# Nine weight slots instead of six in the expert phases of a two-layer decoder step, with the rows fetched on ACT's queue

## The reference, cut to what matters

```python
def hier_moe(x, w_group, b_group, w_router, b_router, w_gate_up, w_down):
...
    def expert_block(a):
        xb, e = a
        gate, up = jnp.split(xb @ w_gate_up[e], 2, axis=-1)
        return (jax.nn.silu(gate) * up) @ w_down[e]
...
    y = jax.ops.segment_sum(yp[dest] * w_sorted[:, None].astype(x.dtype), tok_sorted, num_segments=n)
```

## Time and profile before

| | us |
|---|---|
| timed runs, median of 3 (lowest to highest) | 2165.03 (2158.33 to 2166.91) |
| the profiled execution, first to last instruction | 2143.9 |
| PE busy in it | 1693.2 |
| expert phase of layer 0, first to last product (L883 to L896) | 648.0 to 1207.5 |
| expert phase of layer 1 | 1579.2 to 2109.5 |

### The profile page before, as it was taken

One profiled execution on the slowest core, in us unless ns is written; L12 is line 12 of the kernel. 1 busy time (PEld: TensorE's weight loads), 2 busy tenths in 40 slices (PEclk: granted clock), 3 DMA queues, 4 the chain that ended last, 5 costly groups with the idle time before them and its releaser, 6 DMA issues.

```text
span 2143.9 us, 25298 instructions
## 1 busy us (share of the span) xinstructions
PE 1693.2 (79%) x8325; PEld 773.9 (36%) x8326; DVE 487.7 (23%) x1022; ACT 324.1 (15%) x601; POOL 123.2 (6%) x147
## 2 busy tenths in 40 slices
PE   5989787687937788787887579989757887887782
PEld 3433333344432443333332244434523333322231
DVE  1679244321140110000000132120510000000003
ACT  3022344222020001000110220000210011110001
POOL 0012000120120000000000200001010000000002
PEclk7999888798968999999999879999679998999897
DMA  9951686785048698999999930201569999999995
GB/s 357 416 171 70 216 300 231 239 303 217 0 164 309 243 392 334 395 386 412 411 411 410 364 134 0 79 0 41 196 264 363 361 412 410 411 411 411 411 410 208
DMA packets 194115, 604.27 MB, mean 282 GB/s; under 512 B 15951, under 2 KB 18288, under 8 KB 193897
## 3 DMA queue, kind: packets, MB, share of 16 engines
q1 hardware_dynamic: 162800, 522.55, 62.9%
q10 hardware_dynamic: 21025, 46.17, 5.7%
q0 software_dynamic: 10208, 34.48, 4.5%
HBM read 551.57 MB, written 52.01 MB: 282 GB/s over the span
## 4 chain that ended last, share of the span: by engine, by line
PE 60%; DVE 10%; SPq 8%; DMA 8%; issue 7%; ACT 4%; POOL 1%; ACTq 1%; DVEq 0%; POOLq 0%
PE ps L883 17%; PE ps L896 10%; PE ps L1008 8%; SPq L400 7%; PE ps L578 5%; PE ps L594 3%; DMA ring<-in_w_gate_up_dram 2%; PE ps L928 2%; DMA ring<-in_w_down_dram 2%; PE ps L623 2%; PE ps L940 1%; DVE W L1483 1%; PE ps L906 1%; PE ps L520 1%; PE ps L718 1%
## 5 line engine op out<-in xcount | busy, mean ns | idle before, releaser
L883 PE MATMUL ps<-ring,W 128*64 128x512 f32 x2048 | 470.5, 610 | 55.8 <-issue 32.3
L896 PE MATMUL ps<-ring,W 128*64 128x512 f32 x1024 | 268.1, 670 | 50.3 <-DVE W L1806 48.8
L883 PEld LDWEIGHTS ps<-ring,W 128*64 128x64 f32 x2048 | 173.5, 141 | 341.1 <-issue 341.1
L1033 ACT ACTIVATE W<-ps 128x512 f32<-128x512 f32 (+3 forms) x244 | 138.1, 579 | 901.0 <-PE ps L896 357.0
L1800 DVE TENSOR_TENSOR W<-W,ps 128x256 f32<-128x256 f32 x64 | 27.0, 421 | 798.2 <-ACT W L1334 798.2
L1008 PE MATMUL ps<-hT,ring 128*128 128x512 f32 x384 | 167.5, 596 | 0.0
L896 PEld LDWEIGHTS ps<-ring,W 128*64 128x64 f32 x1024 | 89.5, 152 | 187.3 <-issue 187.2
L1008 PEld LDWEIGHTS ps<-hT,ring 128*128 128x128 f32 x384 | 72.6, 191 | 94.1 <-issue 94.1
L623 PE MATMUL ps<-ring,hT 128*128 128x512 f32 x192 | 88.0, 614 | 1.9 <-DVE W L1498 1.9
L1334 ACT ACTIVATE W<-ps 128x256 f32<-128x256 f32 x64 | 24.5, 383 | 420.5 <-PE ps L883 420.3
L1483 DVE SCALAR_TENSOR_TENSOR W<-W,prm 128x512 f32<-128x512 f32 x116 | 85.3, 804 | 0.0
(11 more groups left out here) (305 smaller groups left out, 1398.7 us busy)
## 6 DMA issues: line engine op xcount, KB each, us to landing
ring<-in_w_gate_up_dram SPq DMA_DIRECT2D x128, 2048.0 KB, 16.6
ring<-in_w_down_dram SPq DMA_DIRECT2D x64, 2048.0 KB, 16.4
ring<-in_w_ada_dram SPq DMA_DIRECT2D x24, 2048.0 KB, 8.9
x_rows<-X ACTq DMA_DIRECT2D x1, 18944.0 KB, 72.4
ring<-in_cache_k_dram SPq DMA_DIRECT2D x64, 256.0 KB, 3.1
W<-x_rows SPq DMA_DIRECT2D x32, 512.0 KB, 16.0
x_rows<-W ACTq DMA_DIRECT2D x128, 128.0 KB, 5.9
ring<-in_cache_v_dram POOLq DMA_DIRECT2D x48, 256.0 KB, 5.4
```

Of the source, the lines that this page charges most:

```text
L883: x = mm(ps[CAP * z:CAP * z + CAP, 2 + j, :], xt[:, k, :], at[:, :, 256 * z:256 * z + 256], start=(k == 0), stop=(k == KD - 1))
L896: x = mm(ps[CAP * z:CAP * z + CAP, 5 + j, :], ht[:, k % 2, CAP * (k // 2):CAP * (k // 2) + CAP], ring[:, 3 * j + 2, at:at + 512], start=(k ...
L1033: return fn(out, src, ACT.Copy, **k)
```

## The change

Nine slots are used in place of six, so three experts are held. The three new slots are not new memory: `Hb`, `hT` and `W` become parts of one tile `M`, and the slots lie over the turned rows and the work area. Slots 7 and 8 can be filled once h is made and the router has read `hT`, and slot 6 once the ranking is done (`bounds`). What the expert phase kept in `W` (rows, turned rows, h and y of an expert) moves to the place of `Hb`, which is free once the rows are scattered. There is room for only one `xg` there, and three pairs of `xT`.

```diff
+M_HB, M_HT, M_W = 0, NT * D, NT * D + KD * T
+M_XG, M_XT, M_Y = M_HB, M_HB + 1024, M_HB + 4096
+M_HH, M_HHT, M_XT2, M_HH2, M_HHT2, M_Y2, M_END = M_HT, M_HT + 512, M_HT + 1024, M_HT + 1280, M_HT + 1408, M_HT + 1536, M_HT + 1792
+M_SLOT = (M_END + SLOT, M_END + 2 * SLOT, M_END)
+W_G2, T_G2S = 8704, 3072
...
         X = sb("X", [P, NT, D])
-        Hb = sb("Hb", [P, NT, D])
-        hT = sb("hT", [P, KD, T])
-        W = sb("W", [P, W_N])
+        M_ = sb("M", [P, M_W + W_N])
+        Hb = M_[:, M_HB:M_HT].rearrange("p (a b) -> p a b", a=NT)
+        hT = M_[:, M_HT:M_W].rearrange("p (c t) -> p c t", c=KD)
+        W = M_[:, M_W:M_W + W_N]
         C = sb("C", [P, NC])
...
+        def slot(s):
+            return ring[:, s, :] if s < NSLOT else M_[:, M_SLOT[s - NSLOT]:M_SLOT[s - NSLOT] + SLOT]
+
         tflat = hT[:, :, :].rearrange("p c t -> p (c t)")
```

```diff
-        def each_expert(eng, step):
-
-            def quad(q, last=False):
-                step(4 * q, 0, 2 * q, 0)
-                step(4 * q + 1, 1, 2 * q, 0, nxt=(1, q, 2 * q + 1))
-                step(4 * q + 2, 0, 2 * q + 1, 1)
-                step(4 * q + 3, 1, 2 * q + 1, 1, nxt=None if last else (0, q + 1, 2 * q + 2))
-
-            with eng.Fori(0, E // 4 - 1) as q:
-                quad(q)
-            quad(E // 4 - 1, last=True)
+        def each_expert(eng, step, between=lambda: None):
+
+            with eng.Fori(0, E // 6) as q:
+                for i in range(0, 6, 2):
+                    p = 3 * q + i // 2
+                    step(6 * q + i, 0, p, i // 2, (i % 3, 2 * q + i // 3), first=True)
+                    step(6 * q + i + 1, 1, p, i // 2, ((i + 1) % 3, 2 * q + (i + 1) // 3), nxt=((i // 2 + 1) % 3, p + 1))
+            between()
+            step(E - 2, 0, PAIRS - 1, 0, (0, E // 3))
+            step(E - 1, 1, PAIRS - 1, 0, (1, E // 3))
```

```diff
+                layer_wait(sp, l, "h_ok", NT)
+                layer_wait(sp, l, "lg_mm", 1)
+                part(2 * EG, 2, 1)
+                part(2 * EG, 2, 2)
+                layer_wait(sp, l, "bounds", 1)
+                part(2 * EG, 2, 0)
+
+                def step(q, i):
+                    n, e = 12 * q + i, EG * ((i + 3) % G) + 3 * q + (i + 3) // G
+                    for k, name in enumerate(("g0_mm", "gu_mm", "down_mm")):
+                        sp.wait_ge(M[name], done(l, n))
+                        part(e, i % 3, k)
+
+                with sp.Fori(0, 2) as q:
+                    for i in range(12):
+                        step(q, i)
+                for i in range(E - 3 - 24):
+                    step(2, i)
```

```diff
-                spread(l, 4, mod(l, 5), 0).then_inc(L["gate2_mm"], 1)
...
+                def second_gate():
+                    pe.wait_ge(M["xa_ok"], pdone(l, PAIRS - 1))
+                    pe.wait_ge(M["xd_ok"], pdone(l, PAIRS - 1))
+                    for c in range(KD):
+                        x = mm(ps[:, c // 4, P * (c % 4):P * (c % 4) + P], mod(l, 5)[:, c, 0:1].to_broadcast([P, P]), ident,
+                               start=True, stop=True)
+                    x.then_inc(L["gate2_mm"], 1)
+                    layer_wait(pe, l, "rep_ok", 4)
+                    layer_wait(pe, l, "gate2_ev", 2)
+                    for c in range(KD):
+                        x = mm(ps[0:NS, c // 4, P * (c % 4):P * (c % 4) + P], w(W_RA, KD, NS)[:, c, :], ident,
+                               start=True, stop=True)
+                    x.then_inc(L["gate2_mm"], 1)
```

```diff
             def ffn(l, k0):
+                def rows_in(p):
+                    act.dma_start(xg, x_dram[bass.ds(P * p, P), :]).then_inc(x_in, 16)
...
-                gates(l, "gate2", w(W_G2, D), tflat[0:NS, 0:D], 0)
+                layer_wait(act, l, "disp", 32 * NT)
+                rows_in(0)
                 meet(act, k0)
...
+                    if first:
+                        carry(act)
+                        rows_in(p + 1)
```

More of the change, by code:

```diff
@@ L161, in hybrid_step, with w @@
         neglam = lamw[:, 4:5]
[L163 to L164 removed]
+        def w(at, *dims, rows=P, of=W, base=0):
+            v = of[0:rows, base + at:base + at + int(np.prod(dims))]
             if len(dims) == 1:
@@ L221, in mod @@
             return modT[:, MODS * KD * l + KD * m:MODS * KD * l + KD * m + KD, :]
-        slot_in = [sem(f"slot_in{s}") for s in range(NSLOT)]
+        slot_in = [sem(f"slot_in{s}") for s in range(NRING)]
         v_in = [sem(f"v_in{j}") for j in range(2)]
@@ L249, in hybrid_step @@
         M = {n: sem("m_" + n) for n in "xt_mm xa_ok xd_ok g0_mm gu_mm silu_ok h_ok ht_mm ht_ok down_mm y_ok".split()}
-        x_in, y_out = ([sem(f"{n}{j}") for j in range(2)] for n in ("x_rows_in", "y_rows_out"))
+        x_in = sem("x_rows_in")
+        y_out = [sem(f"y_rows_out{j}") for j in range(2)]
         y_in = [sem(f"y_pair_in{i}") for i in range(NT)]
@@ L274, in ada_in @@
             return 16 if n < ADA0 else 16 * (n // 4 + 1 + (n % 4 > 0))
-        in1 = [in0[s] + 16 * PAIRS + (32 if s < 2 else 16) for s in range(NSLOT)]
+        in_layer = [16 * len(range(s // 3, E, 3)) for s in range(NRING)]
+        in1 = [in0[s] + in_layer[s] + (32 if s < 2 else 16 if s < NSLOT else 0) for s in range(NRING)]
         base_in = [in0, in1]
@@ L890, in h_turns, with down @@
                     x.then_inc(signal, 1)
-                def down(ht, j, signal):
+                def down(ht, j, group, signal):
                     for k in range(FE // P):
@@ L905, in pair_turns, with step, landed @@
                     for k in range(KD):
-                        x = tr(ps[:, k // 4, P * (k % 4):P * (k % 4) + P], xg[:, lane, P * k:P * k + P], ident)
+                        x = tr(ps[:, k // 4, P * (k % 4):P * (k % 4) + P], xg[:, P * k:P * k + P], ident)
                     x.then_inc(M["xt_mm"], 1)
-                def landed(j, k, p):
-                    pe.wait_ge(slot_in[3 * j + k], p * 16 + (base_in[l][3 * j + k] + 16))
-                def step(n, j, p, lane, nxt=None):
+                def step(n, j, p, lane, home, first=False, nxt=None):
+                    group, turn = home
+                    def landed(k):
+                        pe.wait_ge(slot_in[3 * group + k], turn * 16 + (base_in[l][3 * group + k] + 16))
                     def one_pass(c):
@@ L940, in one_pass @@
                                 x = mm(ps[XC * z:XC * z + XC, 5 + j, 0:256], hhT2[:, k, :],
-                                       ring[:, 3 * j + 2, at:at + 256], start=(k == 0), stop=(k == 3))
+                                       slot(3 * group + 2)[:, at:at + 256], start=(k == 0), stop=(k == 3))
                         x.then_inc(F["products"], 1)
@@ L964, in step @@
                     carry(pe)
-                    down(hhT[:, j], j, M["down_mm"])
-                pair_turns(0, 0, 0)
-                each_expert(pe, step)
+                    down(hhT[:, j], j, group, M["down_mm"])
+                def second_gate():
[11 more added lines that the diff above has]
+                    x.then_inc(L["gate2_mm"], 1)
+                    layer_wait(pe, l, "gate2_ev", 4)
+                pair_turns(0, 0)
+                each_expert(pe, step, second_gate)
             ffn(0, 6)
@@ L1343, in step, with second_gate @@
                     store_rows(act, bass.ds(CAP * n, CAP), yh[:, j, :], y_out[j])
-                pair_turned(0, 0, 0)
-                each_expert(act, step)
+                def second_gate():
+                    for z in range(2):
+                        layer_wait(act, l, "gate2_mm", 1)
+                        copy(w(W_G2 + 512 * z, 512), ps[:, z, :]).then_inc(L["gate2_ev"], 1)
+                    for z in range(2):
+                        layer_wait(act, l, "gate2_mm", 2)
+                        copy(tflat[0:NS, T_G2S + 512 * z:T_G2S + 512 * z + 512], ps[0:NS, z, :]).then_inc(L["gate2_ev"], 1)
+                pair_turned(0, 0)
+                each_expert(act, step, second_gate)
             def combine(l, j):
```

61 lines of the change are left out of this document (32 added, 29 removed).

## The result

The changed kernel takes 2332.68 us (median; 2317.56 to 2342.7) against 2165.05: a ratio of 1.079, 95% interval 1.074 to 1.085. It is slower, as forecast, but by 168 us and not by 41.

A forecast was written before the change was run, and what follows sets the result against it. The two expert phases decide: the DMA engines are slower where no further pieces come, the rest is PE's own chain. 2165 - 32 for the parts + 73 for PE's loop code = 2206 us, own range 2176 to 2245, overall 2128 to 2245.

The forecast's parts named there:

- I take the jumps back in full and half of the rest, 73: PE's longer loop: jumps back to overwritten code cost 42 us, new steps up to 62; 73 us taken in all.
- the upper bound, 104: PE's loop code: the term lies between 0 and 104 us, from 42 for jumps back and 62 for new steps.
- what holds seven holds eight: PE's instruction store: guessed to hold eight blocks; ten in a circle push out one another, but maybe not all.
- one new step in four: PE's loop: of 24 more new steps a layer, one in four stalls at 5.2 us, up to 62 us in all.
- The fast side of the sum, -32: All parts but the loop's code: -31 + 3 - 13 + 9 = -32 us, or 2133.
- Waits for weights, -31: PE in both expert phases: three more slots save 9.5 and 15.3 us of weight waits and 6 of slow products.
- Scatter, +3: Slot 6's load shares the DMA engines with the scatter: between 0 and 5 us a layer, 1.5 taken, +3.
- Rows on ACT's queue, 0: Row fetches issued by ACT one pair ahead, over 20 us before PE turns them: cost 0.
- Table loads, -13: ACT's loop: five trips a layer in place of seven, 4 loads fewer at 1.33 + 2.0 us each, -13 us.
- Second gate, +9: PE alone stands in the gate inside the phase: 6 us a layer, half in layer 1, +9 us.
- The loop is held: Rival: PE's loop is held or its fetches are hidden; 2133 us, 2120 to 2150; chance 0.27.
- Worse than the forecast: Rival: jumps back need two blocks one after the other, new steps stall oftener than one in four; 2260 us; chance 0.08.

The follow-up runs named there:

- the padded kernel: Kernel before, six slots, with 16 never-run products put into each of PE's four loop steps (loop of eight blocks): 2394.51 us, ratio 1.113.
- PE's loop shortened: Changed kernel with the further pieces' code in PE's loop only in the steps this input needs: 2207.69 us, ratio 1.025.
- with both: Changed kernel with the further pieces' code on both PE and ACT only in the steps this input needs: 2151.26 us, ratio 0.997.
- the two pairs of kernels: Nine against six slots, one Silu ahead of ACT's loop: 2131.92 (pieces' code only where needed) against 2156.86 us; with pieces counted by one loop: 2120.21 against 2137.35 us.
- the last two: Nine-slot third version and six-slot kernel before, further pieces counted by one loop on every engine, Silu ahead of ACT's loop in both: 2120.21 and 2137.35 us.
- the longest padding: Kernel before, six slots, with 48 never-run products put into each of PE's four loop steps (loop of ten blocks): 2488.55 us, ratio 1.156.

## Why the prediction was right and wrong

**The step that failed** is "I take the jumps back in full and half of the rest, 73". The mechanism was right and came as described (more blocks in every trip, idle with no releaser). Its size was not, on three counts: 73 us were forecast, and some 178 came.
- A jump back to code that is gone costs 8.8 to 9.4 us of idle at seven of the eight jumps (6.3, ahead of a piece, at the other), and some 1.9 of slow products, not 5.2. I took the price of a new step reached by going forward; no row of before had a jump back to missing code, so even the upper bound, 104, wasn't one.
- Nothing stayed. I guessed that ten blocks in a circle would leave some in place; q8 carried ten in each later trip, and the padded kernel shows that some eight leave next to none, so the guess that what holds seven holds eight is not borne out either. Besides the jumps layer 0 shows 16 stalls of 2 to 4 us, where it had seven before and has five with PE's loop shortened: by these the missing code makes 11 of them, where one new step in four was 6 a layer and I took 3.
- ACT was not looked at. Its loop grew as PE's did. With PE's cured, ratio 1.025, and with both, 0.997: by these ratios PE's code cost some 117 us and ACT's 61 more behind it, with the look-ups that the two edits also take out. 178 stands where I had 73.

**The fast side of the sum, -32,** can be read where both loops are held: some 9 us (0.4%) of it came, or 26 with no table load left.
- Waits for weights, -31: all gone in the changed kernel, but because PE was slow. With the loops held 23.0 us stay in layer 1 (23.8 before) and none in layer 0 (9.5 before). In the two pairs of kernels whose code is nearest to each other the slots save 16 to 19 us of waits and 17 to 25 of time. A head start of 15.3 us came out in one layer of one pair (16.1 in layer 0 of the last two); the other three layers save 2.7 to 9.4.
- Scatter, +3: slot 6 cost 3.9 us in layer 0 and, by the version that loads it later, 4.0 in layer 1, so 8 in all. The bound of 5 a layer held, my 1.5 was too low.
- Rows on ACT's queue, 0: right; 9.0 us to land, no later wait.
- Table loads, -13: 10 and not 14, as said, but worth nothing with six slots, where the DMA engines set the pace. I priced them on PE's chain and had the full windows in the same group of rows. With nine slots and held code the other ten are worth some 17 (by the two intervals, anything from 2 to 32).
- Second gate, +9: 5.5 a layer without the idle of 2.5 behind it, so 11.
- The phases are 1,090 us by the table of before, not 1,093; nothing hangs on it.

**The rivals.** "The loop is held" falls by the queue's 129. "Worse than the forecast" named both causes, two blocks at a jump and more stalls; its working gave 2310 at the far end, and it had 0.08; the measured 2333 lies beyond even that.

## What to carry to other kernels

A loop that is unrolled further to suit more buffers pays for its code on every engine that runs it: count the instruction queues' packets in a later trip of the loop, and if the new loop is longer than any that the trace shows held, test it first with code that never runs. An idle gap on one engine can hide the same gap on another, so after curing one read the others' jumps. A shorter chain is worth something only where the transfers leave room: here one line gave nothing with six slots, where it took 14 loads away, and some 17 us with nine, where it took ten.

## What the runs showed that I had not expected

Sixteen products more in each of the four steps of PE's loop cost 11%, all for code that is jumped over. ACT stops for 10.6 us at a jump back of its loop of six steps, and not once the pieces' code is left out of half of them or more, with packets of 8 KB that make up 0.61 MB in the whole run; nor does it stop when the loop announces its jump back. A single activation ahead of a loop took the table load out of every trip. PE's mean granted clock fell with the stalls, from 0.902 to 0.876 in the changed kernel and 0.848 with the longest padding; gate and up behind a stall took mostly 8.4 to 9.7 us for 7.07 in layer 0, and no run here separates the clock from the stall in that part of the cost.
